# The doubling levels of a chunked RWKV-7 scan: from an unrolled sequence in two quadrants of TensorE to a loop in four, with the transposed inverse by TensorE and ScalarE

## Chip, cores and metric

One Trainium2 chip, one of its cores. The metric is the device time of one execution of the whole kernel in microseconds (us), median over runs.

## What is computed

A two-layer backbone on 512 latent and 256 context tokens of width 1024. Each layer has a token mixer with four head groups and an MLP. One head group is a bidirectional RWKV-7 time mixing: 4 heads of 64, a scan forward and one backward, over all 768 tokens.

```python
def rwkv_scan(S0, r, w, k, v, a, b, reverse):
    def step(S, inp):
        r_t, w_t, k_t, v_t, a_t, b_t = inp
        sa = jnp.einsum('bhij,bhj->bhi', S, a_t)
        S = S * w_t[:, :, None, :] + sa[..., :, None] * b_t[:, :, None, :] + v_t[..., :, None] * k_t[:, :, None, :]
        return S, jnp.einsum('bhij,bhj->bhi', S, r_t)
```

The kernel does this scan in chunks of 64 tokens. Within a chunk, a 64x64 strictly triangular matrix of a against b has to be turned into the inverse of a unit triangular matrix; everything else in the chunk is then products with that inverse.

## The kernel before

The RWKV scan of a layer runs in three visits (`STEPS`, index `s`; `n` counts the visits over both layers, so there are six). A visit handles two halves, `x` = 0 and 1; each half has two directions `g`, four heads (written as `p` and `f`, 2 by 2) and two chunks `c`, so 16 inverses of 64x64 at once. The two chunks `c` lie on partitions 0 to 63 and 64 to 127.

A visit on TensorE, in order: products of keys against a (`paired`, `keyed`, 64 products, issued at the end of the visit before), 24 transposes of keys into token order (L1934, L1943), then the levels, then Z, RM, N, `within`, the state steps and `outputs`.

The inverse is built by doubling. `TN` holds the inverses of the diagonal blocks of size `half` (2, 4, 8, 16, 32 in `LEVELS`), `TT` holds them transposed. A level has, for each half x:

- X: 16 products of the matrix (`ABR`) with the first halves of the columns of `TN`, 32 columns each, into PSUM
- Xm: VectorE masks X from PSUM into `XM` (L1352)
- Tp: 16 products of `TT` with `XM`, 32 columns each, into PSUM
- tn: VectorE adds Tp into `TN` (L1359)
- tt: VectorE transposes the 32x32 blocks of `TN` into `TT` (L1363), all levels but the last

Order on TensorE: X of x=0, X of x=1, Tp of x=0, Tp of x=1. The semaphores are named after the product or the step and its half: `s_X`, `s_Xm`, `s_Tp`, `s_tn`, `s_tt`. In level 1 TensorE also does `seen(x)`, 16 products of 64 columns (AV), which ScalarE copies out (L934, `s_av`, `s_ave`). In the first visit of a layer 12 products for the RWKV bonus stand in level 2 (`s_gate`, `s_bonps`, `s_bon`). The levels are unrolled in the code. A product of fp32 operands is recorded as two weight loads and two matmuls.

X, Tp and `seen` use c alone to choose rows and columns of TensorE: chunk 0 in the upper left quadrant of 64x64, chunk 1 in the lower right. N, `within`, the steps' outputs and the key products go through all four quadrants, in the order `FOUR`:

```python
        FOUR = ((0, 0), (1, 1), (0, 1), (1, 0))
```

Other stages in this text: the MLP is a hardware loop on every engine (`Fori(0, FFG)`, 4 rounds, L2150 on TensorE). `against` fills the products of `paired` and `keyed`.

Of the kernel before, what the change touches and what calls it, by code (L numbers as in the profile page):

```python
# [90 lines left out]
M_ID = M_STEP + 64 * len(LEVELS)  # L91
# [19 lines left out]
def backbone(nc, xT_d, cT_d, pcol_d, constf_d, constm_d, rope_d, wmask_d, wmod_d, win_d, wout_d, w1_d, w2_d,  # L111
             uq_d, ukv_d, w2a2_d, g2_d, ln_d, smask_d, out_d):
    with ExitStack() as ctx:
# [100 lines left out]
        KS, BONUS = 3844, 2048 + 1024 + 256  # L214
# [133 lines left out]
        s_X, s_Xm, s_Tp = pair("s_X"), pair("s_Xm"), pair("s_Tp")  # L348
        s_Z, s_Za, s_Zd = pair("s_Z"), pair("s_Za"), pair("s_Zd")
# [4 lines left out]
        s_seen = sem("s_seen")  # L354
# [303 lines left out]
        def _(act):  # L658
# [38 lines left out]
            for l in range(DEPTH):  # L697
# [212 lines left out]

                nbk = NB if l < DEPTH - 1 else NBL
                t = nbk * P
                for s in range(STEPS):
# [9 lines left out]
                    for x in range(2):  # L923
                        act.wait_ge(s_an[x], n + 1)
                        nc_.activation(cells(-1, HALF[x] + AN, [1, 512]), ps[:, 2048 * x + 512:2048 * x + 1024],
                                       ACT.Copy).then_inc(s_ane[x], 1)
                    if s == 0:
                        act.wait_ge(s_bonin, 2 * (l + 1))
                        for f in range(2):
                            ins = nc_.activation(bonus_in[:, f, :], bonus_in[:, f, :], ACT.Identity, scale=par(l, "r_k", f))  # L930
                        ins.then_inc(s_gate, 1)
                    for x in range(2):
                        act.wait_ge(s_av[x], n + 1)
                        nc_.activation(cells(-1, HALF[x] + AV, [1, 512]), ps[:, 2048 * x + 1536:2048 * x + 2048],  # L934
                                       ACT.Copy).then_inc(s_ave[x], 1)
                    if s == STEPS - 1:
                        for f in OUT_ORDER[0:4]:
                            out_part(f, t)
# [3 lines left out]
                    for x in range(2):  # L942
                        act.wait_ge(s_Z[x], n + 1)
                        nc_.activation(cells(-1, HALF[x] + ZZ, [1, 512]), ps[:, 2048 * x:2048 * x + 512],
                                       ACT.Copy).then_inc(s_Za[x], 1)
# [52 lines left out]
        def _(dve):  # L998
# [96 lines left out]
            for l in range(DEPTH):  # L1095
# [238 lines left out]
                for s in range(STEPS):  # L1334
# [13 lines left out]
                    for j, half in enumerate(LEVELS):  # L1348
                        m = M_STEP + 64 * j
                        for x in range(2):  # L1350
                            dve.wait_ge(s_X[x], 5 * n + j + 1)
                            V.tensor_tensor(cells(-1, HALF[x] + XM, [128, 2], [32, 4], [1, 32]),  # L1352
                                            bank(-1, 2048 * x, [128, 2], [32, 4], [1, 32]),
                                            bass.AP(km, m, [[NKM, P], [32, 2], [0, 4], [1, 32]]),
                                            ALU.mult).then_inc(s_Xm[x], 1)
                        for x in range(2):
                            dve.wait_ge(s_Tp[x], 5 * n + j + 1)
                            t = cells(-1, HALF[x] + TN, [256 + half, 2], [2 * half, 128 // half], [1, half])
                            V.tensor_tensor(t, t, bank(-1, 2048 * x + 1024, [128, 2], [half, 128 // half], [1, half]),  # L1359
                                            ALU.add).then_inc(s_tn[x], 1)  # L1360
                            if j < len(LEVELS) - 1:
                                dve.wait_ge(s_tn[x], 6 * n + j + 2)
                                V.transpose(cells(-1, HALF[x] + TT, [1, 512]),  # L1363
                                            cells(-1, HALF[x] + TN, [1, 512])).then_inc(s_tt[x], 1)
                    for x in range(2):
                        dve.wait_ge(s_Z[x], n + 1)
                        V.tensor_copy(cells(-1, HALF[x] + ZZ + 512, [1, 512]),
                                      ps[:, 2048 * x + 512:2048 * x + 1024]).then_inc(s_Zd[x], 1)
# [92 lines left out]
        def _(pe):  # L1461
# [108 lines left out]
            for l in range(DEPTH):  # L1570
# [319 lines left out]
                for s in range(STEPS):  # L1890
# [56 lines left out]
                    def seen(x):  # L1947

                        h, o = HALF[x], 2048 * x + 1536
# [10 lines left out]
                    for j, half in enumerate(LEVELS):  # L1960
                        for x in range(2):
                            h, o = HALF[x], 2048 * x
                            pe.wait_ge(s_tn[x], 6 * n + j + 1)
                            for g in range(2):
                                for p in range(2):
                                    for f in range(2):
                                        for c in range(2):
                                            ins = mm(bank(c, o + g * P + (2 * p + f) * 32, [1, 32]),
                                                     cells(c, h + ABR + p * 512 + f * 256 + g * P, C1),
                                                     cells(c, h + TN + g * (256 + half) + (2 * p + f) * 64,  # L1970
                                                           [2 * half, 32 // half], [1, half]))
                            ins.then_inc(s_X[x], 1)
                        if s == 0 and j == 2:
                            pe.wait_ge(s_gate, 2 * l + 2)
                            for b in range(NB):
                                for f in range(2):
                                    c = BONUS + b * 4 + 2 * f
                                    ins = mm(ps[:, c:c + P], bonus_in[:, f, b * P:(b + 1) * P], halves)
                            ins.then_inc(s_bonps, 1)
                        for x in range(2):  # L1980
                            h, o = HALF[x], 2048 * x + 1024
                            pe.wait_ge(s_Xm[x], 5 * n + j + 1)
                            if j == 0:
                                pe.wait_ge(s_ke[x], n + 1)
                            else:
                                pe.wait_ge(s_tt[x], 4 * n + j)
                            if s == 0 and j == 2 and x == 1:
                                pe.wait_ge(s_bon, l + 1)
# [300 lines left out]
```

## Time and profile before

| | |
|---|---|
| time, median of 3 runs | 2339.92 us (2337.46 to 2340.94) |
| the profiled execution: its own time, its span | 2341.85 us, 2340.0 us |
| busy in the span: PE, PE weight loads, DVE, ACT, POOL | 2182.5, 1772.0, 965.5, 663.5, 772.4 us |
| granted clock of TensorE over the span | 0.97 |
| PE in the chain that ended last | 82% |
| one visit of the scan (the second of layer 0) | 44.46 us |

In the profile PE is TensorE's matmuls and PEld its weight loads, which overlap them; DVE is VectorE, ACT ScalarE, POOL GpSimd. A visit is read from the trace by its first X product: 558.18 us for the second visit of layer 0 and 602.64 us for the third.

### The profile page before, as it was taken

Reading aid. Unit: us, or ns where it says so; the run is one execution under the profiler, and the core shown is the slowest. Engines: PE = TensorE matmul, PEld = TensorE weight load, DVE = VectorE, ACT = ScalarE, POOL = GpSimd, SP = SyncE. Lnnn points to the kernel's source line nnn. Section 1 sums busy time; section 2 is a strip of 40 time slices with the busy share of each in tenths; the row PEclk is TensorE's granted clock in tenths of the full one; section 3 lists DMA queues with packets and bytes.
Section 4 is the critical chain, followed back from the end, with each engine's and each line's share of the span. In section 5 each row is a group of like instructions: output and inputs, shape, how many; then the busy total and the mean of one; then the engine's idle time right before and its main releaser. Section 6 shows DMA issues by size and latency. Waiting matters only on the chain.

```text
span 2340.0 us, 44960 instructions
## 1 busy us (share of the span) xinstructions
PE 2182.5 (93%) x19332; PEld 1772.0 (76%) x19332; DVE 965.5 (41%) x1474; ACT 663.5 (28%) x1166; POOL 772.4 (33%) x546
## 2 busy tenths in 40 slices
PE   5999999989888999999999899999989988999997
PEld 3888577669875888888888578847759965888886
DVE  3002355476735622314141420235476646452452
ACT  3100366642312211111021221046642223221221
POOL 3333243032231223232323243235214142444443
PEclk9999999989999999999999989999979999999998
DMA  7221200120122122222213231120120033333331
GB/s 266 76 78 55 72 2 2 60 73 4 34 62 100 53 63 63 63 63 63 63 63 134 99 114 51 44 73 1 61 72 4 4 99 118 98 93 97 95 94 63
DMA packets 45434, 163.24 MB, mean 70 GB/s; under 512 B 5505, under 2 KB 5505, under 8 KB 45025
## 3 DMA queue, kind: packets, MB, share of 16 engines
q1 hardware_dynamic: 44480, 158.29, 20.9%
q8 instruction: 124, 2.03, 0.4%
q0 software_dynamic: 800, 2.69, 0.3%
q14 instruction: 30, 0.24, 0.0%
HBM read 158.86 MB, written 2.10 MB: 69 GB/s over the span
## 4 chain that ended last, share of the span: by engine, by line
PE 82%; DVE 9%; ACT 5%; issue 2%; DMA 1%; POOL 0%; SPq 0%; POOLq 0%; ACTq 0%; DVEq 0%
PE ps L1463 78%; PE ps L1780 3%; ACT flat L781 1%; DVE part_h L1072 1%; DVE xT L1090 1%; DVE hT L1065 1%; DVE flat L1088 1%; DMA flat<-wmod_dram 1%; PE ps L2049 0%; DVE flat L1447 0%; ACT flat L795 0%; DVE part_h L1332 0%; ACT hT L795 0%; DVE flat L1256 0%; DVE flat L1312 0%
## 5 line engine op out<-in xcount | busy, mean ns | idle before, releaser
L1463 PE MATMUL ps<-part_hi,wparts 128*128 128x512 f32 (+1 forms) x3072 | 824.3, 355 | 20.9 <-DVE part_h L1072 9.6
L1463 PEld LDWEIGHTS ps<-part_hi,wparts 128*128 128x128 f32 x3072 | 548.0, 191 | 111.8 <-DVE part_h L1072 12.5
L535 POOL TENSOR_TENSOR wparts<-flat,wparts 128x1024 fp32r<-128x1024 f32 x184 | 446.4, 2426 | 524.5 <-ACT wparts L987 518.7
L1463 PE MATMUL ps<-part_h,wparts 128*128 128x512 f32 (+1 forms) x1536 | 544.5, 354 | 0.0
L1463 PE MATMUL ps<-flat 64*64 64x32 f32 (+8 forms) x8200 | 428.3, 257 | 23.3 <-DVE flat L1277 10.6
L1463 PE MATMUL ps<-part_mlp,wparts 128*128 128x512 f32 (+1 forms) x1536 | 415.3, 357 | 13.2 <-DVE part_h L1072 7.6
L1463 PEld LDWEIGHTS ps<-flat 64*64 64x64 f32 (+4 forms) x8200 | 332.6, 141 | 106.2 <-issue 73.0
L1463 PEld LDWEIGHTS ps<-part_h,wparts 128*128 128x128 f32 x1536 | 295.3, 192 | 40.1 <-issue 1.7
L1463 PEld LDWEIGHTS ps<-part_mlp,wparts 128*128 128x128 f32 x1536 | 275.5, 191 | 57.2 <-POOL wparts L535 9.9
L987 ACT ACTIVATE wparts<-flat 128x1024 fp32r<-128x1024 f32 x112 | 118.9, 1062 | 694.9 <-PE ps L1463 694.9
L1463 PE MATMUL ps<-part_lo,wparts 128*128 128x512 f32 (+1 forms) x768 | 272.2, 354 | 0.0
L532 POOL CAST wparts<-flat 128x1024 fp32r<-128x1024 f32 x72 | 77.7, 1079 | 513.9 <-PE ps L1463 196.1
L1447 DVE TENSOR_TENSOR flat<-flat 128x768 f32<-128x768 f32 (+1 forms) x64 | 158.6, 2479 | 210.8 <-ACT flat L991 210.3
L1454 DVE TENSOR_TENSOR flat<-flat,ps 128x768 f32<-128x768 f32 (+1 forms) x64 | 52.6, 821 | 353.7 <-PE ps L1463 353.7
L1463 PEld LDWEIGHTS ps<-part_lo,wparts 128*128 128x128 f32 x768 | 145.2, 189 | 20.0
L730 ACT ACTIVATE flat<-ps 128x768 f32<-128x768 f32 (+1 forms) x40 | 30.8, 770 | 309.2 <-PE ps L1463 309.2
L1780 PE MATMUL ps<-kf,flat 128*128 128x128 f32 x592 | 90.4, 283 | 14.9 <-ACT flat L781 10.0
L781 ACT ACTIVATE flat<-ps,small 128x768 f32<-128x768 f32 (+2 forms) x120 | 93.8, 785 | 29.8 <-DVE small L1172 29.8
L1780 PEld LDWEIGHTS ps<-kf,flat 128*128 128x128 f32 x592 | 64.6, 141 | 40.4 <-ACT flat L781 22.8
L1132 DVE RECIPROCAL small<-small 128x48 f32<-128x48 f32 x2 | 0.9, 452 | 208.7 <-ACT small L736 208.7
L1463 PE MATMUL ps<-flat,silu 128*32 128x512 f32 x352 | 54.8, 730 | 30.2 <-DMA flat<-wmod_dram 28.7
L1172 DVE TENSOR_REDUCE small<-ps 128x1 f32<-128x768 f32 (+1 forms) x80 | 65.9, 847 | 30.2 <-PE ps L1463 30.0
(206 smaller groups left out, 2027.5 us busy)
## 6 DMA issues: line engine op xcount, KB each, us to landing
flat<-w_dram SPq DMA_DIRECT2D x128, 512.0 KB, 3.5
flat<-wmod_dram SPq DMA_DIRECT2D x88, 512.0 KB, 5.6
flat<-win_dram SPq DMA_DIRECT2D x40, 512.0 KB, 3.5
flat<-wout_dram SPq DMA_DIRECT2D x16, 512.0 KB, 3.6
hT<-wmod_dram SPq DMA_DIRECT2D x8, 512.0 KB, 8.2
xT<-xT_dram SPq DMA_DIRECT2D x8, 384.0 KB, 6.6
flat<-rope_dram SPq DMA_DIRECT2D x2, 1024.0 KB, 5.6
out_dram<-xT SPq DMA_DIRECT2D x8, 256.0 KB, 2.0
```

Source lines behind the costliest of these rows:

```text
L532: ch.link(pool.tensor_copy(whi[q % 2], src))
L535: pool.tensor_tensor(wlo[q % 2], src, whi[q % 2], ALU.subtract).then_inc(s_used[q], 1)
L730: nc_.activation(zv[:, tile, 0:t], ps[:, (q % 2) * 1024:(q % 2) * 1024 + t], ACT.Copy).then_inc(s_ev, 1)
L781: nc_.activation(prob[:, h % 2, 0:w], ps[:, (h % 2) * 1024:(h % 2) * 1024 + w], ACT.Exp, bias=small[:, h:h + 1], scale=-1.0 if h >= 8 else ...
L987: nc_.activation(whi[q % 2], slab[:, q * SLAB:(q + 1) * SLAB], ACT.Copy).then_inc(s_whi, 1)
L1065: ins = V.scalar_tensor_tensor(out=hv[:, k, a:b], in0=xv[:, k, a:b], scalar=gains[:, l, which, k, s:s + 1], in1=rs[:, a:b], op0=ALU.mult, ...
L1072: ins = V.scalar_tensor_tensor(out=pre_lo[:, k - 1, a:b], in0=hv[:, k - 1, a:b], scalar=mods[:, l, 12 * which + k - 1, s:s + 1], in1=pre_h ...
L1172: V.tensor_reduce(nm, src, AX.X, ALU.max, negate=True).then_inc(s_nm, 1)
L1447: ch.link(V.tensor_tensor(raw, raw, raw, ALU.mult))
L1454: V.tensor_tensor(yT[:, k, 0:t], yT[:, k, 0:t], ps[:, o:o + t], ALU.add).then_inc(s_ev2, 1)
L1463: return pe.matmul(out, lhsT, rhs, start=start, stop=stop)
L1780: ins = pe.transpose(ps[:, c:c + P], prob[:, h % 2, k * P:(k + 1) * P], ident)
```

## The change

- The five levels become one hardware loop on TensorE (`pe.Fori`), with the same 96 products in each round. Waits in it compare with a register, and each pair of such waits is followed by an increment of an unused semaphore.
- X, Tp and a new product run through four quadrants. In X and the new product the heads with p = 1 change from the rows of chunk c to the columns of the other chunk, so their results lie on the other half of the partitions; Tp turns them back.
- X computes all 64 columns (before: the 32 of the first halves). VectorE's mask (Xm) then takes the columns that it needs, in two instructions for each half x (p = 0 and 1), as does the addition (tn).
- `TT` is made by TensorE and ScalarE: 16 products of `TN` with the identity (`s_tr`), copied from PSUM by ScalarE (`transposed`, L914 of the changed kernel, `s_tt`), in every level. VectorE's block transpose is gone.
- `seen` for both halves and the bonus products stand behind the loop. ScalarE copies a half's token keys and a half's token a by turns.
- In the third visit ScalarE's four `out_part` copies stand between its `transposed` copies.

```diff
@@ constants @@
-M_ID = M_STEP + 64 * len(LEVELS)
+M_ID = M_STEP + P * len(LEVELS)
...
@@ ScalarE @@
+                def transposed(n, j):
+
+                    for x in range(2):
+                        act.wait_ge(s_tr[x], 5 * n + j + 1)
+                        nc_.activation(cells(-1, HALF[x] + TT, [P, 2], [256, 2], [1, P]),
+                                       bank(-1, 2048 * x + 1280, [512, 2], [P, 2], [1, P]), ACT.Copy).then_inc(s_tt[x], 1)
+
...
-                    if s == 0:
-                        act.wait_ge(s_bonin, 2 * (l + 1))
-                        for f in range(2):
-                            ins = nc_.activation(bonus_in[:, f, :], bonus_in[:, f, :], ACT.Identity, scale=par(l, "r_k", f))
-                        ins.then_inc(s_gate, 1)
+                    for j in range(len(LEVELS)):
+                        transposed(n, j)
+                        if s == 0 and j == 0:
+                            act.wait_ge(s_bonin, 2 * (l + 1))
...
+                        if s == STEPS - 1 and j < 4:
+                            out_part(OUT_ORDER[j], t)
@@ VectorE @@
                         for x in range(2):
                             dve.wait_ge(s_X[x], 5 * n + j + 1)
-                            V.tensor_tensor(cells(-1, HALF[x] + XM, [128, 2], [32, 4], [1, 32]),
-                                            bank(-1, 2048 * x, [128, 2], [32, 4], [1, 32]),
-                                            bass.AP(km, m, [[NKM, P], [32, 2], [0, 4], [1, 32]]),
-                                            ALU.mult).then_inc(s_Xm[x], 1)
+                            for p in range(2):
+                                ins = V.tensor_tensor(cells(-1, HALF[x] + XM + p * P, [64, 2], [half, 64 // half], [1, half]),
+                                                      bank(-1, 2048 * x + p * 512, [128 + half, 2],
+                                                           [2 * half, 64 // half], [1, half]),
+                                                      bass.AP(km, m, [[NKM, P], [64, 2], [half, 64 // half], [1, half]]),
+                                                      ALU.mult)
+                            ins.then_inc(s_Xm[x], 1)
...
-                            if j < len(LEVELS) - 1:
-                                dve.wait_ge(s_tn[x], 6 * n + j + 2)
-                                V.transpose(cells(-1, HALF[x] + TT, [1, 512]),
-                                            cells(-1, HALF[x] + TN, [1, 512])).then_inc(s_tt[x], 1)
@@ TensorE @@
-                    for j, half in enumerate(LEVELS):
+                    with pe.Fori(0, len(LEVELS)) as j:
                         for x in range(2):
                             h, o = HALF[x], 2048 * x
-                            pe.wait_ge(s_tn[x], 6 * n + j + 1)
+                            pe.wait_ge(s_tn[x], j + (6 * n + 1))
+                            pe.sem_inc(s_sawslab, 1)
+                            pe.wait_ge(s_ke[x], n + 1)
                             for g in range(2):
-                                for p in range(2):
-                                    for f in range(2):
-                                        for c in range(2):
-                                            ins = mm(bank(c, o + g * P + (2 * p + f) * 32, [1, 32]),
-                                                     cells(c, h + ABR + p * 512 + f * 256 + g * P, C1),
-                                                     cells(c, h + TN + g * (256 + half) + (2 * p + f) * 64,
-                                                           [2 * half, 32 // half], [1, half]))
+                                for f in range(2):
+                                    for p, c in FOUR:
+                                        ins = mm(bank(c ^ p, o + 1280 + p * 512 + g * P + f * 64, C1),
+                                                 cells(c, h + TN + g * 256 + (2 * p + f) * 64, C1),
+                                                 kf[64 * c:64 * c + 64, K_ID * P + 64 * c:K_ID * P + 64 * c + 64])
+                            ins.then_inc(s_tr[x], 1)
+                            pe.wait_ge(s_ane[x], n + 1)
+                            for g in range(2):
+                                for f in range(2):
+                                    for p, c in FOUR:
+                                        ins = mm(bank(c ^ p, o + p * 512 + g * P + f * 64, C1),
+                                                 cells(c, h + ABR + p * 512 + f * 256 + g * P, C1),
+                                                 cells(c, h + TN + g * 256 + (2 * p + f) * 64, C1))
                             ins.then_inc(s_X[x], 1)
...
                         for x in range(2):
                             h, o = HALF[x], 2048 * x + 1024
-                            pe.wait_ge(s_Xm[x], 5 * n + j + 1)
...
+                            pe.wait_ge(s_tt[x], j + (5 * n + 1))
+                            pe.wait_ge(s_Xm[x], j + (5 * n + 1))
+                            pe.sem_inc(s_sawslab, 1)
                             for g in range(2):
...
+                                for f in range(2):
+                                    for p, c in FOUR:
+                                        ins = mm(bank(c, o + p * 512 + g * 64 + f * 32, [1, 32]),
+                                                 cells(c ^ p, h + TT + g * 256 + (2 * p + f) * 64, C1),
+                                                 cells(c ^ p, h + XM + p * P + g * 64 + f * 32, [1, 32]))
                             ins.then_inc(s_Tp[x], 1)
-                            if j == 1:
-                                seen(x)
+                    for x in range(2):
+                        seen(x)
...
                     for x in range(2):
                         h, o = HALF[x], 2048 * x
                         pe.wait_ge(s_tn[x], 6 * n + 6)
-                        pe.wait_ge(s_ane[x], n + 1)
+                        pe.wait_ge(s_ave[x], n + 1)
```

TensorE at the start of the levels of the first visit, before: the first two levels up to `seen` of x=0, each group with the semaphores that it waits for.

```order
L1463 MATMUL ps<-flat 64x32 [waits s_tn0]
L1463 MATMUL ps<-flat 64x32 x15
L1463 MATMUL ps<-flat 64x32 [waits s_tn1]
...
L1463 MATMUL ps<-flat 64x32 [waits s_ke0,s_Xm0]
...
L1463 MATMUL ps<-flat 64x32 [waits s_ke1,s_Xm1]
...
L1463 MATMUL ps<-flat 64x32 [waits s_tt0,s_Xm0]
...
L1463 MATMUL ps<-flat 64x64 [waits s_akm0]
L1463 MATMUL ps<-flat 64x64 x15
```

The same place of the changed kernel: the whole body of the loop, from the branch into it to the compare and branch at its end, and what follows it. The first product of each half is now the one with the identity (`kf`).

```order
L1968 UNCONDITIONAL_BRANCH
L1968 ISA
L1471 MATMUL ps<-kf,flat 64x64 [waits s_tn0,s_ke0]
L1471 MATMUL ps<-kf,flat 64x64 x15
L1471 MATMUL ps<-flat 64x64 [waits s_ane0]
L1471 MATMUL ps<-flat 64x64 x15
...
L1471 MATMUL ps<-flat 64x32 [waits s_tt0,s_Xm0]
L1471 MATMUL ps<-flat 64x32 x15
...
L1968 COMPARE_AND_BRANCH
L1471 MATMUL ps<-flat 64x64 [waits s_akm0]
```

A round has six groups of 16 products instead of four, and `seen` moved from the second level to behind the last.

VectorE in one level of the first visit, before:

```order
L1352 TENSOR_TENSOR flat<-ps,km 128x256 [waits s_X0]
L1352 TENSOR_TENSOR flat<-ps,km 128x256 [waits s_X1]
L1359 TENSOR_TENSOR flat<-flat,ps 128x2x64x2 [waits s_Tp0]
L1363 STREAM_TRANSPOSE flat<-flat 128x512 [waits s_tn0]
L1359 TENSOR_TENSOR flat<-flat,ps 128x2x64x2 [waits s_Tp1]
L1363 STREAM_TRANSPOSE flat<-flat 128x512 [waits s_tn1]
```

and after:

```order
L1360 TENSOR_TENSOR flat<-ps,km 128x128 [waits s_X0]
L1360 TENSOR_TENSOR flat<-ps,km 128x128
L1360 TENSOR_TENSOR flat<-ps,km 128x128 [waits s_X1]
...
L1370 TENSOR_TENSOR flat<-flat,ps 128x2x32x2 [waits s_Tp0]
L1370 TENSOR_TENSOR flat<-flat,ps 128x2x32x2
L1370 TENSOR_TENSOR flat<-flat,ps 128x2x32x2 [waits s_Tp1]
```

Each addition and each mask is two instructions of half the width, and the block transposes are gone from the level.

ScalarE of the changed kernel around the first round of the first visit; before, the two copies of `s_kt` stood ahead of the two of `s_an`, and no instruction of ScalarE belonged to a level:

```order
L927 ACTIVATE flat<-ps 128x1024 [waits s_kt0]
L930 ACTIVATE flat<-ps 128x512 [waits s_an0]
L927 ACTIVATE flat<-ps 128x1024 [waits s_kt1]
L930 ACTIVATE flat<-ps 128x512 [waits s_an1]
L914 ACTIVATE flat<-ps 128x2x2x128 [waits s_tr0]
L914 ACTIVATE flat<-ps 128x2x2x128 [waits s_tr1]
L937 ACTIVATE flat<-flat,pcol 128x768 [waits s_bonin]
```

Ten `transposed` copies a visit are new on ScalarE.

## Rows read from the trace of the kernel before

**Rows 1.** The page: busy time by engine; the chain by engine.

```profile
PE 2182.5 (93%) x19332; PEld 1772.0 (76%) x19332; DVE 965.5 (41%) x1474; ACT 663.5 (28%) x1166; POOL 772.4 (33%) x546
PE 82%; DVE 9%; ACT 5%; issue 2%; DMA 1%; POOL 0%; SPq 0%; POOLq 0%; ACTq 0%; DVEq 0%
```

**Rows 2.** Windows: length, busy of each engine, clock; level stages, one rest.

```profile
558.18:579.06 20.88, 20.77 (x705) 20.66 (x705) 14.18 (x29) 2.36 (x5) 4.34 (x7) 1.00 0.02 4
579.06:602.64 23.58, 19.67 (x673) 18.13 (x669) 16.35 (x24) 9.48 (x20) 8.16 (x6) 1.00 0.01 3
602.64:623.50 20.86, 20.86 (x710) 20.86 (x710) 13.78 (x29) 5.29 (x9) 0.00 (x0) 1.00 0.02 5
```

**Rows 3.** Windows: one level, N, and between two stalls of TensorE.

```profile
573.00:576.74 3.74, 3.74 (x135) 3.74 (x132) 2.87 (x7) 0.00 (x0) 0.00 (x0) 1.00 0.02 4
584.60:586.30 1.70, 1.70 (x128) 1.70 (x122) 1.70 (x4) 0.59 (x1) 1.20 (x3) 1.00 0.04 10
588.47:592.57 4.10, 2.54 (x128) 2.40 (x128) 2.12 (x4) 0.00 (x0) 0.50 (x1) 1.00 0.01 4
558.18:602.64 44.46, 40.44 (x1370) 38.79 (x1369) 30.53 (x53) 11.85 (x25) 12.51 (x13) 1.00 0.02 4
```

**Rows 4.** Timeline of VectorE in one level: start, length, instruction, idle before.

```profile
573.00 0.39 DVE L1352 TENSOR_TENSOR flat<-ps,km 128x256 f32<-128x256 f32 x1
573.66 0.42 DVE L1352 TENSOR_TENSOR flat<-ps,km 128x256 f32<-128x256 f32 x1 [0.27 <-PE ps L1463]
574.62 0.42 DVE L1359 TENSOR_TENSOR flat<-flat,ps 128x256 f32<-128x256 f32 x1 [0.53 <-PE ps L1463]
```

**Rows 5.** Timeline of `within` and the steps: TensorE without a releaser, four quadrants.

```profile
588.47 0.46 PE L2049 MATMUL ps<-flat 64*64 64x64 f32 x17 [1.19 <-issue]
...
589.12 1.07 PEld L2049 LDWEIGHTS ps<-flat 64*64 64x64 f32 x63
...
592.57 0.50 PE L2060 MATMUL ps<-flat 64*64 64x64 f32 x17 [1.56 <-issue]
```

**Rows 6.** DMA queues, 558.18 to 602.64: packets, MB, share; then 896 to 1300.

```profile
q8 instruction: 10, 0.16, 1.5%
...
q1 hardware_dynamic: 8007, 29.13, 23.0%
```

**Rows 7.** Windows: the first two rounds of layer 0's MLP loop.

```profile
749.80:896.20 146.40, 138.75 (x771) 121.12 (x771) 65.07 (x74) 29.35 (x38) 44.21 (x20) 0.97 0.24 73
896.20:1029.70 133.50, 133.50 (x770) 117.99 (x769) 40.21 (x32) 20.45 (x22) 40.37 (x18) 1.00 0.21 63
```

**Rows 8.** Groups by line: VectorE at 128 columns, ScalarE at 512, VectorE's transposes.

```profile
L1198 DVE TENSOR_TENSOR hT<-ps,flat 128x128 f32<-128x128 f32 x60 | 17.5, 292 | 76.5 <-ACT flat L802 53.7 <-PE ps L1463 22.8
L944 ACT ACTIVATE flat<-ps 128x512 f32<-128x512 f32 x12 | 7.2, 598 | 73.6 <-PE ps L1463 73.6
L1363 DVE STREAM_TRANSPOSE flat<-flat 128x512 f32<-128x512 f32 x48 | 34.1, 711 | 1.6
```

**Rows 9.** Timeline where the second visit's levels begin.

```profile
558.18 1.01 PEld L1463 LDWEIGHTS ps<-flat 64*64 64x64 f32 x32 [0.17 <-issue]
558.25 1.09 ACT L925 ACTIVATE flat<-ps 128x512 f32<-128x512 f32 x2
558.64 0.71 DVE L1347 STREAM_TRANSPOSE flat<-flat 128x512 f32<-128x512 f32 x1
559.35 0.42 DVE L1352 TENSOR_TENSOR flat<-ps,km 128x256 f32<-128x256 f32 x1
559.40 24.00 PEld L1463 LDWEIGHTS ps<-flat 64*64 64x64 f32 x768 [0.22 <-DVE flat L1347]
```

**Rows 10.** Timeline, first visit: the bonus products, their copy, level 2 behind them.

```profile
522.39 3.30 PEld L1463 LDWEIGHTS ps<-kf,flat 128*128 128x128 f32 x24
525.98 0.19 ACT L941 ACTIVATE bon<-ps 128x24 f32<-128x24 f32 x1 [4.71 <-PE ps L1463]
```

More of the change, by code:

```diff
@@ L347, in backbone @@
         s_av, s_ave = pair("s_av"), pair("s_ave")
-        s_X, s_Xm, s_Tp = pair("s_X"), pair("s_Xm"), pair("s_Tp")
-        s_Z, s_Za, s_Zd = pair("s_Z"), pair("s_Za"), pair("s_Zd")
+        s_X, s_Xm, s_Tp, s_tr = pair("s_X"), pair("s_Xm"), pair("s_Tp"), pair("s_tr")
+        s_Z, s_Ze = pair("s_Z"), pair("s_Ze")
         s_RM, s_R, s_N, s_Ne = pair("s_RM"), pair("s_R"), pair("s_N"), pair("s_Ne")
@@ L1356, in _ @@
                         for x in range(2):
                             dve.wait_ge(s_Tp[x], 5 * n + j + 1)
[L1358 to L1364 removed]
+                            for p in range(2):
+                                t = cells(-1, HALF[x] + TN + p * P, [256 + half, 2], [2 * half, 64 // half], [1, half])
+                                ins = V.tensor_tensor(t, t, bank(-1, 2048 * x + 1024 + p * 512, [64, 2],
+                                                                 [half, 64 // half], [1, half]), ALU.add)
@@ L1980, in _ @@
                         for x in range(2):
                             h, o = HALF[x], 2048 * x + 1024
-                            pe.wait_ge(s_Xm[x], 5 * n + j + 1)
[L1983 to L1988, printed above, removed]
-                            for g in range(2):
-                                for p in range(2):
-                                    for f in range(2):
-                                        for c in range(2):
-                                            ins = mm(bank(c, o + g * P + (2 * p + f) * 32, [1, 32]),
-                                                     cells(c, h + TT + g * 256 + (2 * p + f) * 64, C1),
-                                                     cells(c, h + XM + g * P + (2 * p + f) * 32, [1, 32]))
@@ new lines, in _ @@
+                            ins.then_inc(s_Tp[x], 1)
+                    for x in range(2):
+                        seen(x)
+                    if s == 0:
+                        pe.wait_ge(s_gate, 2 * l + 2)
+                        for b in range(NB):
+                            for f in range(2):
+                                c = BONUS + b * 4 + 2 * f
+                                ins = mm(ps[:, c:c + P], bonus_in[:, f, b * P:(b + 1) * P], halves)
+                        ins.then_inc(s_bonps, 1)
```

39 lines of the change are left out of this document (16 added, 23 removed).

## The prediction

> **What bounds the kernel now.** I read the page first. TensorE has 82% of the chain that ended last; VectorE is busy 41% of the span [rows 1]. So what the change takes from VectorE (its transposes, 34.1 us in all [rows 8]) is worth only what TensorE waits for it. I then cut a visit into stages by windows. The level stage, from the first X product to the first Z product, takes 20.88 us, and 20.86 in the third visit (two of six shown; the first visit of each layer has the bonus products besides) [rows 2]. TensorE loads weights through 20.66 of the 20.88. The rest of the visit takes 23.58 and the change hardly touches it. In a level TensorE has no gap: 3.74 us, loads for 3.74 [rows 3], while VectorE idles before each mask and addition (0.27, 0.53) until TensorE is done [rows 4]. The levels are bound by TensorE.
>
> By what on TensorE? A level is 64 products with two loads each, 128 loads in 3.74 us: 29.2 ns a load. These use two quadrants. Where the kernel uses four, 63 loads took 1.07 us [rows 5]: less the last load's own 0.13, 0.94/62 = 15 ns. N (four quadrants too) shows about the same, 122 loads touched in 1.70 us [rows 3]. The change's products have 64 or 32 columns, as the rows of N and of the levels have, so I take 15 ns a load and 0.47 us for a group of 16 products, against 0.935 in two quadrants.
>
> A second limit stands behind. TensorE twice stops in the fast stage with nothing to wait for (1.19 and 1.56, "issue") [rows 5]. Between the two restarts lie 4.10 us with 128 loads and 128 matmuls [rows 3]. In the whole visit there are 1369 loads, 1370 matmuls, and 10 packets of 16 KB on the instruction queue [rows 3, 6]. So a packet holds about 256 instructions, and TensorE can't take one faster than in some 4 us when it runs straight on. The levels now, 256 instructions in 3.74 us, are just at that rate. Four quadrants in unrolled code would gain little; the loop is what could let them.
>
> **The loop's instructions.** A round has 96 products, 384 loads and matmuls, with the control some 400 instructions: parts of two or three packets. The MLP's loop has 770 loads a round [rows 7], over 1500 instructions. Yet from 896 to 1300, three rounds, the instruction queue isn't among the queues that moved anything [rows 6], and later rounds take 133.50 [rows 7] without a stop. So a loop of six packets is kept, and rounds 2 to 5 here should fetch nothing.
>
> **One round, step by step.** Time 0 is the first load of the transposes (tr). tr and X of half 0 issue until 0.94, tr and X of half 1 until 1.88. From a group's last issue to its reader on VectorE take 0.24 us, my estimate from the level's rows: the mask at 573.66 stands behind an X group that fills 573.0 to 573.43. A VectorE instruction on 128 columns is 0.29 us [rows 8]; a pair of them, slightly overlapped, 0.52.
>
> - Xm of half 0: 1.18 to 1.70. `TT` of half 0: ScalarE from 0.71 for 0.60 [rows 8]. Tp of half 0 can follow X at once, 1.88 to 2.35.
> - Xm of half 1: 2.12 to 2.64. Tp of half 1: from about 2.8 (the wait is released before the increment and the load, so 0.1 beyond the usual 0.05) to 3.27.
> - tn of half 0: VectorE from 2.64 to 3.16, before TensorE could be back.
> - Back edge: no row shows its price, since the MLP hides it. Lower bound 0; upper bound the larger of the release gaps here, 0.22 [rows 9], taken three times for branch, register wait and increment, 0.66. I take the middle, 0.33.
>
> That makes 3.6 us a round against 3.74: two quadrants' 128 loads become four quadrants' 192, 2.82 us of issue, and the remaining 0.8 is waiting that did not exist before. VectorE's and ScalarE's share (2.1 and 1.2) is no bound.
>
> **First round.** tn of half 1 comes at 559.35, as before [rows 9]. Only then can tr and X of half 1 go (559.5 to 560.5, where X alone took 559.40 to 560.34), and the rest of the round follows: 4.05 us, as now (3.74 plus the gap). ScalarE's new order, keys and `an` by turns, makes its copy for half 1 end near 559.65, no later than X needs it. But this round runs through new code. The code of a visit shrinks by some 1290 instructions for the levels and grows by 400, so where the body begins in a packet differs from visit to visit; counting on from the stops in the trace I find that in five of six visits it touches a third packet. That comes about 4 us after the second was entered, near 4.2, and is needed in the second Tp, near 3.4. I charge 0.8 in those five; in the first visit nothing.
>
> **After the last round.** The last Tp issues until 3.27, the exit 0.15, `seen` of half 0 is 0.935, and its copy by ScalarE 0.24 + 0.60 + 0.15. Z can begin there; `seen` of half 1 lies beside it. In the first visit of a layer the bonus (3.30) stands behind `seen`, and Z now waits for its copy (0.19 and two hand-overs, some 0.5), where before it ran while the levels went on [rows 10].
>
> **Sum for a visit.** 4.05 + 3 x 3.60 + 3.27 + 0.15 + 0.935 + 0.99 = 20.2 against 20.88: 0.7 less. Six visits: -4.2. Fetch in five first rounds: +4.0. Bonus in two visits: +0.35 each, as part of the copies is covered: +0.7. ScalarE's `out_part` copies (768 columns, under 0.9 each by the 512 of [rows 8]) in the third visit lie between tt and the next tr, covered by 1.3 us of slack; if not, they cost some 0.7 x 4 in each of two visits, in no case of mine likely. Sum +0.5: the profiled span 2340.0 becomes 2340.5. The profiled execution took 2341.85, 1.9 above the median 2339.92, so the median to be expected is 2340.4.
>
> **The page against the row.** The Trainium skill (Runtime: NRT & Kernel Launch, Instruction fetch mechanics) says that fetching is sequential in a window of two pages and that a taken branch out of it must fetch its target before going on. By it every back edge of a body over three pages would stop for a fetch; by the MLP's rows none does. The price is the fourth rival's.
>
> **Rivals.**
> 1. Rounds quicker (0.20). The back edge hides behind the 3.27 of issue and the first round's third packet is early. Then 24 later rounds at 3.35 give 6 more, the fetch 4 more: 2330.5. For it: the MLP's back edges cost nothing visible.
> 2. Rounds slower (0.21). Register waits stop TensorE's sequencer, so that nothing stands ready behind them: 0.1 to 0.15 for each of the four, rounds of 4.0: 24 x 0.4 = +9.6, 2350. The point of decision is a round of 3.8 us: above it the levels lose. For it: six groups a round where there were four, each shorter than the hand-over behind it (0.24 + 0.52).
> 3. A fetch under way delays the first back edge (0.08). The third packet's entry starts the fetch of a fourth, just before the branch. If the branch waits for that, near 3.5 us in each of five visits: +17, 2358.
> 4. Nothing is kept of a body that touches three packets (0.04): two fetches a round at 4 us instead of 3.6 in all, 24 x 4.4 = +106, 2446. Against it, rows 6 and 7.
> 5. The four quadrants don't run side by side (0.02), since in tr, X and Tp both row halves write to one bank. Six groups at 0.935 make 5.6 us a round: 30 x 1.9 = +57, 2397. Against it: the `within` products (L2049) do the same at 15 ns a load [rows 5]. The Trainium skill (TensorEngine Tiling (Array Packing), Restrictions and Gotchas) says that different row tiles can't use a bank at once; the row disagrees.
> 6. The loads saved shift the fetch stops of the fast stage favourably or not; that is inside the range, two stops of 1.2 to 1.6 a visit, of which one may come or go.
>
> **How the numbers follow.** The forecast has 0.45. A measurement of this kernel can tell about 0.2%, 4.7 us. Its own spread (a round 3.5 to 3.7, a fetch 0 to 1.5) is +-5. Faster by over 0.2%: rival 1 and the forecast's edge, 0.22. Slower: rivals 2 to 5 less what of 2 stays under 4.7, and an edge of the forecast, 0.34. Within: 0.44. The range goes from rival 1's 2330.5 rounded down to just above rival 2: 2330 to 2353.
>
> **What would show it.** Rounds: VectorE's masks for half 0 recur every 3.6 us in rounds 2 to 5, with an idle stretch before tr of the next round. Loads in tr, X and Tp 15 ns apart. Seven or eight packets of 16 KB a visit instead of 10 or 11, none in rounds 2 to 5. First round near 4.9 where it touches three packets. The first Z 20.2 to 21 us after the first load. The prediction is wrong if rounds are under 3.4 or over 3.8, if a stop of some 4 us appears at a back edge, or if the 23.58 us behind the levels move by more than 1.

## The result, and the profile after

The changed kernel takes 2354.01 us (5 runs, 2351.49 to 2355.49); the kernel before, on the same chip, 2340.94 (5 runs, 2337.46 to 2344.95). The ratio is 1.0057, 95% interval 1.0046 to 1.0069: 13 us slower, where 2340.4 was forecast and 2353 was the upper end of the range.

The page of the kernel after, profiled at 2355.49 us, in the order of [rows 1] and [rows 6]: TensorE (PE), the instruction queue (packets, MB, share), the chain by engine, and the group of the MLP's products.

```profile
span 2353.7 us, 49101 instructions
PE 2169.6 (92%) x21252; PEld 1754.9 (75%) x21252; DVE 943.0 (40%) x1546; ACT 698.6 (30%) x1226; POOL 773.5 (33%) x546
...
q8 instruction: 130, 2.13, 0.4%
...
PE 81%; DVE 10%; ACT 5%; issue 3%; POOL 1%; DMA 0%; SPq 0%; POOLq 0%; ACTq 0%; DVEq 0%
...
L1471 PE MATMUL ps<-part_mlp,wparts 128*128 128x512 f32 (+1 forms) x1536 | 421.4, 361 | 27.4 <-issue 13.0
```

TensorE is busy for 13 us less than before, and the kernel is slower: what it lost is waiting, and the page names the kind. "Issue", time in which the engine waited for nothing that is recorded, rose in the chain from 2% to 3%, and 13.0 of the 27.4 us that TensorE sat idle ahead of the MLP's products is of that kind.

Windows of the scan, layer 0: the level stage of the second visit, the rest of that visit, the level stage of the third, and the second visit whole. They answer to [rows 2] and the last of [rows 3].

```profile
555.53:575.75 20.22, 18.21 (x1023) 17.25 (x1024) 10.70 (x42) 8.00 (x14) 4.32 (x7) 1.00 0.01 2
575.75:598.92 23.17, 19.79 (x674) 18.27 (x670) 15.92 (x23) 9.80 (x21) 8.15 (x6) 1.00 0.02 4
598.92:618.90 19.98, 17.99 (x1019) 17.13 (x1020) 10.31 (x41) 10.75 (x18) 0.00 (x0) 1.00 0.01 2
555.53:598.92 43.39, 38.00 (x1690) 35.53 (x1689) 26.62 (x65) 17.80 (x35) 12.47 (x13) 1.00 0.01 3
```

The level stages take 20.22 and 19.98 us where they took 20.88 and 20.86; the forecast was 20.2, and 21.0 with the third packet's 0.8, which both of these visits have. The visit is 1.07 us shorter. The scan gained more than was forecast, so the loss is elsewhere. The next three windows are the second, third and fourth round of layer 0's MLP loop, cut at its back edges; before, the second was 133.50 [rows 7].

```profile
894.05:1034.96 140.91, 136.56 (x770) 120.23 (x768) 40.25 (x32) 20.45 (x22) 40.35 (x18) 0.98 0.19 61
1034.96:1175.48 140.52, 136.19 (x771) 119.96 (x769) 40.24 (x32) 20.46 (x22) 40.35 (x18) 0.98 0.19 61
1175.48:1315.74 140.26, 135.93 (x770) 119.71 (x769) 40.24 (x32) 25.72 (x29) 47.37 (x22) 0.98 0.25 88
```

Each is some 7 us longer, with the same work: 21 us in a loop that the diff does not touch. Two views of the same place say what happens there. First the timeline of TensorE behind the back edge at 894.05 (start, length, instruction, idle before it), then the DMA queues from 898 to 1320.

```profile
898.17 0.47 PE L1471 MATMUL ps<-part_mlp,wparts 128*128 128x512 f32 x1 [2.01 <-issue]
898.48 0.40 PE L1471 MATMUL ps<-part_h,wparts 128*128 128x512 f32 x1
901.21 0.80 PE L1471 MATMUL ps<-part_mlp,wparts 128*128 128x512 f32 x2 [2.34 <-issue]
```

```profile
q1 hardware_dynamic: 7920, 28.84, 20.3%
q8 instruction: 26, 0.43, 0.4%
```

In these rounds 26 packets of 16 KB of instructions were fetched; before, the instruction queue isn't among the queues that moved anything there [rows 6]. The loop is fetched again in every round. The instructions of the loop's own line show it most plainly, first after, then before (durations in ns: lowest, median, highest; the first and last start).

```profile
L2161 PEldq COMPARE_BRANCH  x4: 76/3764/3851, 894.0 to 1315.7; - x4
```

```profile
L2150 PEldq COMPARE_BRANCH  x4: 76/208/214, 896.2 to 1296.9; - x4
```

The branch back took 0.21 us before and takes 3.8 us after (the 76 ns is the exit, not taken back). TensorE's matmuls stand still for 2.01 us of it, and behind it comes the second stop of 2.34 us.

The stops are not the whole price. The first of the three rounds is 7.41 us longer than the 133.50 before: 4.35 are these two stops, and 3.06 are TensorE's busy time, 136.56 against 133.50 for the same work. The granted clock shows where they lie: from 901.20 to 905.50, right behind the second stop, it is 0.50, the lower of its two levels (1.2 GHz), from 905.50 to 910 0.81, and 1.00 for the rest of the round. Before, it was 1.00 through this round [rows 7].

### The profile page after: what moved, and what is told of

It is laid out like the page before. It is cut to its first block, busy times and chain, and to the rows that moved or that the text cites. A ratio compares the mean times of both kernels' runs of the same rounds, so it can differ in the third digit from the quotient of the medians.

```text
span 2353.7 us, 49101 instructions
## 1 busy us (share of the span) xinstructions
PE 2169.6 (92%) x21252; PEld 1754.9 (75%) x21252; DVE 943.0 (40%) x1546; ACT 698.6 (30%) x1226; POOL 773.5 (33%) x546
## 4 chain that ended last, share of the span: by engine, by line
PE 81%; DVE 10%; ACT 5%; issue 3%; POOL 1%; DMA 0%; SPq 0%; POOLq 0%; ACTq 0%; DVEq 0%
PE ps L1471 76%; PE ps L1788 3%; DVE part_h L1079 1%; ACT flat L780 1%; DVE hT L1072 1%; DVE xT L1097 1%; DVE flat L1095 1%; POOL flat L553 1%; DVE part_h L1339 1%; PE ps L2060 0%; DVE flat L1455 0%; ACT flat L794 0%; DVE flat L1360 0%; ACT hT L794 0%; DMA xT<-xT_dram 0%
## 5 line engine op out<-in xcount | busy, mean ns | idle before, releaser
L1471 PE MATMUL ps<-part_mlp,wparts 128*128 128x512 f32 (+1 forms) x1536 | 421.4, 361 | 27.4 <-issue 13.0
L1471 PE MATMUL ps<-flat 64*64 64x64 f32 (+8 forms) x8200 | 387.9, 256 | 30.5 <-DVE flat L1284 9.6
L1471 PEld LDWEIGHTS ps<-flat 64*64 64x64 f32 (+4 forms) x8200 | 287.1, 141 | 114.6 <-issue 82.6
L1471 PE MATMUL ps<-kf,flat 64*64 64x64 f32 (+3 forms) x2312 | 90.8, 229 | 7.4 <-ACT flat L833 3.4
L1471 PEld LDWEIGHTS ps<-kf,flat 64*64 64x64 f32 (+1 forms) x2312 | 83.7, 144 | 15.0 <-ACT flat L833 5.0
```

The source lines that it names most:

```text
L1471: return pe.matmul(out, lhsT, rhs, start=start, stop=stop)
```

## The theory, its rival and the experiments

Theory: TensorE's instructions come in packets of 256. Layer 0's MLP loop has 1572 instructions. It is kept while it touches seven packets and fetched anew each round when it touches eight. Seven packets hold 1792 instructions, so it is kept if it begins in places 0 to 220 of a packet, and lost in 221 to 255. The diff takes some 900 instructions a visit from the code ahead of that loop, three visits in layer 0; in the two programs the loop's places differ by 117, modulo 256, and I counted 130 before and 247 after. (My first count had both 32 lower, at 98 and 215; the runs with N = 148 and 116 below moved it, and those with 84, 96, 6 and 12 came after.) The 1572 and the 117 are counts of the programs' instructions and stand in no view; the edges found below are their test. Rivals: the new loops themselves, or the register waits, leave something behind that slows what follows; or the loss is one of the scan's, and the MLP's stops only come with it.

All kernels below that differ only in the place of the loop have this edit, with N idle increments of a semaphore that nobody waits for:

```diff
+                if l == 0:
+                    for _ in range(N):
+                        pe.sem_inc(s_sawslab, 1)
                 with pe.Fori(0, FFG) as i:
```

**The changed kernel with N = 16** (to place 7 of the next packet).

> The changed kernel with 16 increments of an unused semaphore on TensorE ahead of layer 0's MLP loop, nothing else. Theory (place of the MLP loop): TensorE's instructions come in packets of 256; the MLP loop of layer 0 has 1572 instructions, and the change moved its start so far into a packet that its body and the packet ahead no longer stay in the buffer, so each of its 3 back edges stops for two fetches, 7 us each. Then moving it on by 16, past the next packet's start, gives the 21 us back: 2333 us, later MLP rounds of 133.5 us, no instruction packets in rounds 2 to 4. Rival (the levels' loop itself, or its register waits, costs the time, or transfers collide): 16 cheap instructions change nothing, 2354 us.

2333.69 us (12 runs, 2332.81 to 2338.36) against 2340.48 for the kernel before (19 runs), ratio 0.9978, interval 0.9969 to 0.9988. Sixteen instructions that do nothing take 20.3 us off the changed kernel (2354.01 less 2333.69; the kernel before, measured beside each of the two, differed by 0.5), and it is then faster than before. The windows of the same three rounds, and the branch of the loop's line:

```profile
892.09:1025.65 133.56, 133.56 (x770) 118.09 (x769) 40.22 (x32) 20.43 (x22) 40.34 (x18) 1.00 0.19 63
1025.65:1159.24 133.59, 133.59 (x771) 118.13 (x770) 40.21 (x32) 20.43 (x22) 40.34 (x18) 1.00 0.19 63
1159.24:1292.77 133.53, 133.53 (x770) 118.05 (x769) 40.21 (x32) 25.68 (x29) 47.37 (x22) 1.00 0.27 91
```

```profile
L2164 PEldq COMPARE_BRANCH  x4: 76/208/213, 892.1 to 1292.8; - x4
```

The three rounds sum to 400.68 against 421.69 above: 21.0 us, the whole difference. The instruction queue has 103 packets in the whole run instead of 130; 26 of the 27 are those seen above.

**The kernel before with N = 148** (place 22 of the next packet).

> The kernel before with 148 such increments ahead of layer 0's MLP loop, which puts its start as far into a packet as the changed kernel has it. Theory: the scan is untouched, and the time rises by 3 x 7 = 21 us, to 2362 us, with stops of about 3.7 us at the back edges. Rival: no change but the price of the increments, at most 5 us, 2341 to 2346 us.

A miss: 2346.4 us (2344.78 to 2352.78), ratio 1.0033, interval 1.0016 to 1.0049. The branches stayed at 0.21 us and the queue at 124 packets. The edit does not do what its expectation says. The two programs' places differ by 117, so 116 increments put the old kernel's loop where the changed kernel's stands (the next run), and 148 push it 31 further, through the bad places and out again; the number rested on a place of the kernel before that was 32 too low. What the increments did cost is their own price. The list of TensorE's waits has it as one wait (us in total, times, longest):

```profile
PE ps L1463 <- issue: 24.1, 4, 21.0
```

148 increments in 21.0 us: 0.14 us each (116 in 16.0 us in the next run). Only 6 of the 21 us show in the time. This run also takes away a rival: more instructions or a pause ahead of the loop don't cost the stops.

**The kernel before with N = 116** (place 246, almost where the changed kernel stands).

> The kernel before with 116 increments. By the counts between stops the MLP loop's body would still lie in seven packets (start at 214 of 256, 1572 instructions, end at 1786 of 1792), just not reaching the eighth. If the limit is the packets of the body alone: back edges without a stop, rounds of 133.5 us, 2341 us. If the instructions after a jump, or a read ahead of some 32 instructions, count too: stops as with 148, 2362 us. The changed kernel, whose count gives nearly the same start (215) and which stops, speaks for the second.

2362.37 us in one run, as the second of the two expectations has it. The old kernel, with the levels unrolled and without a register wait, shows the loss:

```profile
q8 instruction: 151, 2.47, 0.5%
```

```profile
L2153 PEldq COMPARE_BRANCH  x4: 76/3626/4033, 899.2 to 1319.0; - x4
```

So neither the new loop nor the register waits are needed for it. 151 packets less 124 is 27, as between 130 and 103.

**The kernel before with N = 84 and N = 96**, for the edge.

> The kernel before with 84 increments ahead of layer 0's MLP loop. 116 of them stopped at every back edge and 148 did not, so a packet begins some 32 instructions ahead of where I had counted it: the loop starts at 130 of 256 in the kernel before, at 246 with 116 (stops), at 22 of the next with 148 (none), at 247 in the changed kernel (stops), at 7 with its 16 (none). A body of 1572 touches seven packets if it starts at 220 or before. 84 puts it at 214: no stops, rounds of 133.5 us, 2341 to 2345 us. Rival (a window of nearness to a packet's end decides, say the last 50): also none here, so the run with 96 tells the two apart.

> As with 84, but the start is at 226 of 256, so the body touches an eighth packet by 6 instructions. Theory (eight packets of body are one too many): three back edges with stops, 2359 to 2363 us, packets on the instruction queue in rounds 2 to 4. Rival (only the last packets' end matters): none, 2345 us.

84: 2342.97 us, with the kernel before at 2338.02 beside it; branches 0.21, 124 packets. 96: 2355.36 us, branches of 4.6 to 4.7 us, 151 packets, and rounds in between:

```profile
895.47:1033.46 137.99, 135.19 (x771) 119.25 (x770) 40.21 (x32) 20.44 (x22) 40.33 (x18) 0.99 0.21 62
1033.46:1170.80 137.34, 133.94 (x770) 118.11 (x769) 40.22 (x32) 20.44 (x22) 40.33 (x18) 1.00 0.21 62
```

Twelve increments decide over 12 us. The time is below the 2359 to 2363 expected, some 4.3 us a round and not 7. The timelines show what differs at the first back edge. From place 226, with 30 of the loop's instructions in its first packet, TensorE stops once, for 2.80 us. From 246 (N = 116, 10 instructions) it stops for 1.71 and 2.25, from 247 (the changed kernel, 9) for 2.01 and 2.34, from 253 (N = 6 below, 3) once for 5.19. The fewer instructions there are in the first packet, the longer it stands; that they cover part of the next fetch is my reading. The clock has a part too: with N = 96 it fell behind the first back edge (0.61 over 4.1 us) and not behind the second (1.00), whose round is the shorter.

**The changed kernel with N = 6 and N = 12**, for the other edge (places 253 and 3).

> The changed kernel with 6 instead of 16 idle semaphore increments ahead of layer 0's MLP loop. By the theory that the loop is kept only where its 1572 instructions touch seven packets of 256, it now begins 253 instructions into a packet and still touches eight: the stops at its three back edges stay, 2353 to 2357 us, and the instruction queue has some 130 packets. By the rival, that any small shift or pause ahead of the loop mends it, 2333 to 2336 us.

> The same with 12 increments. By the theory of packets the loop begins 3 instructions into the next packet and touches seven: no stops at its back edges, 2332 to 2337 us, the instruction queue at some 103 packets. By the rival, that the cost falls in proportion to the shift, it lies between the result of 6 and that of 16, some 2338 us.

6: 2358.57 us, a little above the 2353 to 2357 expected. 12: 2334.43 us, measured beside it, with the kernel before at 2337.08. The branches of the one and the other:

```profile
L2164 PEldq COMPARE_BRANCH  x4: 76/3363/3667, 897.5 to 1319.8; - x4
```

```profile
L2164 PEldq COMPARE_BRANCH  x4: 76/208/213, 892.6 to 1293.3; - x4
```

Six more instructions are worth 24 us. There is no slope between: 12 does as well as 16, and 6 no better than 0. If the places are s before and s + 117 after, then "84 kept, 96 lost" puts s in 125 to 136 and "6 lost, 12 kept" puts s + 117 in 244 to 249, thus s in 127 to 132. The count of 130 lies in both, and packets of 256 with a limit of seven fit all nine kernels (N = 0, 84, 96, 116 and 148 before; 0, 6, 12 and 16 after).

All nine have the same body of 1572 instructions, so that it touches an eighth packet and that its back edge lies in the first 35 places of a packet are the same thing here. What speaks for the number of packets are the other loops. Layer 1's MLP loop is half as long (386 weight loads a round, not 770), and its branches took at most 0.22 us in every kernel, those that lost layer 0's loop too. The new loops, of two or three packets, took at most 0.23 us in all 30 branches of each kernel that has them. No run varies the length alone.

**The changed kernel with the rounds written out**, without register waits and their increments.

> The changed kernel with its five rounds written out (same products, same waits, no register waits and no increments). A level is then 388 instructions, 1.5 packets. Theory (TensorE takes a packet in 3.6 to 4.1 us when it runs straight on): 5.5 to 6.2 us a level instead of 3.45, 20 to 27 us more in three visits of... 24 later rounds: +50 to +65 us, against which stand the 21 us of the MLP loop if its start falls well (my count puts it at 24 to 60 of 256, so it does): 2385 to 2400 us. Rival (the loop costs as much as it saves, its back edges and register waits): 2330 us, levels of 3.3 us.

```diff
-                    with pe.Fori(0, len(LEVELS)) as j:
+                    for j in range(len(LEVELS)):
...
-                            pe.sem_inc(s_sawslab, 1)
```

2397.19 us (2392.93 to 2401.7), ratio 1.0249, interval 1.0229 to 1.027; as expected. VectorE's masks of half 0 stand 5.4 us apart on average in layer 0, a little under the 5.5 to 6.2 expected. A line of its list of waits, and four rows of its timeline in the second visit:

```profile
PE ps L1471 <- issue: 50.5, 44, 1.9
```

```profile
573.98 0.91 PE L1471 MATMUL ps<-flat 64*64 64x64 f32 x49 [1.34 <-issue]
...
577.77 0.50 PE L1471 MATMUL ps<-flat 64*64 64x64 f32 x17 [1.22 <-issue]
...
581.28 0.48 PE L1471 MATMUL ps<-flat 64*64 64x32 f32 x19 [0.93 <-issue]
...
585.25 1.01 PE L1471 MATMUL ps<-flat 64*64 64x64 f32 x53 [1.82 <-issue]
```

TensorE restarts after 3.79, 3.51 and 3.97 us: the pace of the packets, as in the old fast stage [rows 3, 5]. 2397.19 less 2333.69 is 63.5 us that the loop form saves over the same products in straight code (of which the MLP's loop, kept here with branches of 0.21 us, is no part). The new round in straight code, four quadrants and the added transposes together, would have made the kernel slower; it pays only because rounds 2 to 5 fetch nothing. Four quadrants without the transposes, in straight code, were not run.

**X ahead of the transposes**, in the changed kernel with N = 16: the products of tr move behind those of X in both halves, so that the mask can begin sooner.

> after_pad16 with X ahead of the transposes in both halves of a round; same instructions otherwise. Theory of the round (its length is set by the chain from the last reader of half 1 to Tp of half 1, then the back edge): now the transposes of half 1 end last, ScalarE's copy of 0.60 behind them stands in place of VectorE's masks of 0.49, so rounds grow from 3.45 to about 3.55 us, +2.4 us in all, 2336 us. Rival (a round is bound by TensorE's 192 loads and its control instructions): rounds stay at 3.45.

```diff
+                            pe.wait_ge(s_ane[x], n + 1)
+                            for g in range(2):
...
+                            ins.then_inc(s_X[x], 1)
                             pe.wait_ge(s_ke[x], n + 1)
                             for g in range(2):
...
                             ins.then_inc(s_tr[x], 1)
-                            pe.wait_ge(s_ane[x], n + 1)
-                            for g in range(2):
...
-                            ins.then_inc(s_X[x], 1)
```

2343.44 us in one run (the kernel before beside it: 2338.02), 10 above the median of N = 16 and 7 more than expected. Timeline of TensorE in its second visit, and windows of the same stretch: the first round with its stop, the second, and the third:

```profile
559.54 0.54 PE L1471 MATMUL ps<-flat 64*64 64x32 f32 x21 [0.36 <-ACT flat L914]
561.00 0.42 PE L1471 MATMUL ps<-flat 64*64 64x32 f32 x11 [0.92 <-issue]
561.61 1.11 PE L1471 MATMUL ps<-flat 64*64 64x64 f32 x32 [0.19 <-issue]
...
568.71 0.67 PE L1471 MATMUL ps<-flat 64*64 64x32 f32 x32
...
572.35 0.67 PE L1471 MATMUL ps<-flat 64*64 64x32 f32 x32
```

```profile
554.76:561.50 6.74, 5.03 (x203) 4.18 (x201) 3.73 (x10) 3.56 (x6) 5.54 (x9) 1.00 0.01 2
561.50:565.50 4.00, 3.90 (x160) 3.92 (x160) 1.42 (x6) 0.79 (x2) 0.00 (x0) 0.57 0.00 0
565.50:569.00 3.50, 3.11 (x196) 2.95 (x188) 1.95 (x8) 1.10 (x3) 0.00 (x0) 1.00 0.00 0
```

Now Tp waits for ScalarE's `transposed` copy (L914), which starts a group later. A later round is 3.6 to 3.75 us (the first Tp at 568.71 and at 572.35: 3.64) instead of 3.48 on average, and not the 3.55 that was expected: 24 rounds by 0.17 is 4 us. The second window shows something else: behind the two stops (0.36 and 0.92 us, with little between them) the granted clock stands at 0.57, so mostly at 1.2 GHz, and a group of 32 matmuls lasts 1.11 us instead of 0.68; the second round took over a microsecond longer. This does not tell the two kernels apart, though: N = 16 has such a stretch as well, in the first visit of layer 1, behind a stop of 1.06 us and one of 0.28 (groups of 32 in 1.15 us, a granted clock of 0.73 from 1755 to 1759). The rest of the 10 us is not located. By its rounds the order of the change, transposes first, is the better one, and its mask doesn't wait for ScalarE.

## Why the prediction was wrong, point by point

The forecast was +0.5 us; measured were +13.1. The runs split this: with the MLP's loop kept, the scan and all else gave 6.8 us (2340.48 to 2333.69), and the loss of that loop took 20.3.

- *What bounds the levels*: right. With weight loads at twice the rate in a kept loop the level stage fell by 0.66 and 0.88 us, though a round now issues half as many again. The second limit, fetching, was right too: written out, a round took 5.4 us.
- *Four quadrants at 15 ns a load*: right. The groups tr, X and Tp issue 32 matmuls in 0.47 us, and rival 5 (quadrants in turn) is out. Timeline of TensorE, second round of the second visit in the kernel after:

```profile
560.22 0.69 PE L1471 MATMUL ps<-kf,flat 64*64 64x64 f32 x32 [0.19 <-issue]
560.71 0.68 PE L1471 MATMUL ps<-flat 64*64 64x64 f32 x32
561.17 0.68 PE L1471 MATMUL ps<-kf,flat 64*64 64x64 f32 x32
561.64 1.12 PE L1471 MATMUL ps<-flat 64*64 64x64 f32 x64
562.96 0.67 PE L1471 MATMUL ps<-flat 64*64 64x32 f32 x32 [0.21 <-DVE flat L1360]
```

- *One round, 3.6 us*: the mechanism right, the size 0.12 too long. VectorE's timeline has the masks of half 0 (every fourth pair) at 561.44 and 564.88, 3.44 apart; over all six visits they are 3.44 to 3.64 apart from round 2 on, 3.48 on average.

```profile
561.44 0.49 DVE L1360 TENSOR_TENSOR flat<-ps,km 128x128 f32<-128x128 f32 x2 [0.89 <-PE ps L1471]
562.37 0.49 DVE L1360 TENSOR_TENSOR flat<-ps,km 128x128 f32<-128x128 f32 x2 [0.44 <-PE ps L1471]
562.83 0.48 DVE L1370 TENSOR_TENSOR flat<-flat,ps 128x128 f32<-128x128 f32 x2
563.69 0.49 DVE L1370 TENSOR_TENSOR flat<-flat,ps 128x128 f32<-128x128 f32 x2 [0.38 <-PE ps L1471]
564.88 0.49 DVE L1360 TENSOR_TENSOR flat<-ps,km 128x128 f32<-128x128 f32 x2 [0.70 <-PE ps L1471]
```

  A pair takes 0.49, not the 0.52 I took. Tp of half 1 begins 2.74 after the round's first load (2.8 forecast), and from there to the next round's first load it is 0.70, 0.87 and 0.71 (0.80 forecast, with 0.33 for the back edge from no row). The round lies between the forecast and rival 1 (3.35), and 24 later rounds by 0.12 are 2.9 us. Rivals 2 (rounds of 4.0) and 3 (a stop at the new loop's back edge) did not come: its branches take 0.21 us.
- *The first round, 4.05 and 0.8 for the third packet*: right in size where the stop comes, wrong in how often. The masks of half 0 of rounds 1 and 2 stand 4.68 us apart in the second visit of the kernel after, with the stop inside the second Tp, where it was put. But only three of the six visits are like this (4.68, 4.56 and 4.33 apart), where five were charged; in the other three it is 3.46 to 3.88.

```profile
559.61 0.42 PE L1471 MATMUL ps<-flat 64*64 64x32 f32 x11 [0.45 <-issue]
```

- *Seven or eight packets a visit*: right, 7 on the instruction queue from 555.53 to 598.92, where there were 10 [rows 6].
- *"The rest of the visit takes 23.58 and the change hardly touches it"*: 23.17, 0.4 less. If the other visits did the same (I read the one), that is 2.5 us of the gain that the sum did not have.
- *"So a loop of six packets is kept"*: **this step failed**, though not for the loop I used it for. The rows behind it were of the MLP's loop: 770 loads and 770 matmuls a round, kept, in one position. With its control the loop has 1572 instructions, 6.1 packets; it touches seven in most places and eight in 35 of 256, and that is where it stops being kept. I wrote in the next paragraphs that a visit's code shrinks by 1290 and grows by 400 instructions, "so where the body begins in a packet differs from visit to visit", and followed that only to the new loops. The same shift moves every loop behind the scan. Asked of the MLP's loop, the step would have given 117 places of shift. What a lost loop costs the runs show: 4.35 us of stops at a back edge and 3 us of lower clock behind it, three times.
- *Rival 4* (nothing kept of a body that touches three packets) was the right mechanism in the wrong loop and at the wrong size. The Trainium skill (Runtime: NRT & Kernel Launch, Instruction fetch mechanics) describes a window of two pages, out of which a taken branch must fetch its target first. I weighed the rule against [rows 6, 7] and set it aside for all sizes. The runs show both: branches of 0.21 us with nothing fetched at seven packets and below, against the two pages; branches of 3.4 to 4.7 us at eight, which is the stall that the page describes. The same section of the Trainium skill gives TensorE's instruction memory as 128 KiB, 2048 instructions, thus eight of its pages, which the forecast did not weigh against the two. The runs agree with eight better: seven packets of body are kept and eight are not. That the eighth page is taken by the one fetched ahead would fit, and no run here shows it.
- *Rival 6* took fetch stops for something of the fast stage, within +-3 us. *The sum* missed the scan by 7.3 us (+0.5 forecast, -6.8 measured), in the terms above, each too long or charged too often; and it had no term for the MLP, where 20.3 us were lost; *the range* had its upper end from rival 2, a mechanism that did not occur, and missed by 1 us what it had no case for.

## What to carry to other kernels

A change that adds or removes instructions moves every hardware loop behind it on the same engine. Before it is judged, look at the branches back of those loops and at the instruction queue in their later rounds: a queue that was silent there and now moves packets is a loop that no longer fits. A few idle instructions ahead of it can mend this (here 12, for 20 us), and the measured worth of the edit itself (here -6.8 us) is seen only then.

## What the runs showed of the hardware

- Straight code of short products is bound by fetching: a packet of 256 instructions for every 3.5 to 4.0 us, against 3.48 us for a whole round of some 400 instructions in a kept loop.
- A loop of 1572 instructions is kept where it touches seven packets of 256. Where it touches an eighth, it is fetched whole again (8 or 9 packets a round) and waits 3.4 to 4.7 us at the branch. One edge of the bad places is bracketed to within six instructions (N = 6 and 12), the other to within twelve (84 and 96).
- An idle semaphore increment on TensorE costs 0.14 us, though most of it was hidden here.
- Stops of TensorE cost more than their length where the clock falls behind them. Behind the two stops at the MLP's back edge (2.01 and 2.34 us) the granted clock was 0.50 for 4.3 us; behind 0.36 and 0.92 us, with X first, it was 0.57 over 4 us; behind 1.06 and 0.28 us, with N = 16, 0.73 over 4 us. Behind 0.21 and 0.72 us, in the second visit of N = 16, it stayed at 1.00.
